# Row lists brought back in two parts by four transfers each, GpSimd's six positions nested, and the expert banks cleared ahead of the lists

## The reference, cut to what matters

```python
def moe_ffn(h, router_w, router_b, e_w_in, e_b_in, e_w_out, e_b_out):
    logits = xt @ router_w + router_b              # 32 experts
    top_v, top_i = lax.top_k(logits, 4)
    gates = jax.nn.softmax(top_v, axis=-1)
    # for every expert e, for the rows that chose it:
    #   hh = x @ e_w_in[e] + e_b_in[e];  gate, up = split(hh)
    #   act = min(gate, 7) * sigmoid(1.702 * min(gate, 7)) * (clip(up, -7, 7) + 1)
    #   y[row] += gate_of_row * (act @ e_w_out[e] + e_b_out[e])
x = layer_norm(alpha * x + mix);  x = layer_norm(alpha * x + moe_ffn(x))
```

## Time and profile before

| what | value |
|---|---|
| time, median of 3 runs | 1468.83 us (1467.07 to 1471.85) |
| time of the profiled execution | 1466.7 us |
| its span, first to last instruction | 1464.9 us |
| busy: PE / DVE / ACT / POOL | 1257.5 / 508.6 / 180.6 / 317.5 us |
| mean granted TensorE clock | 0.919 |
| DMA, mean over the span | 315 GB/s |

### The profile page before, as it was taken

The page is one execution under the profiler, slowest core; times in us unless marked ns, Lnnn a source line. Parts: engine busy times, 40 slices in busy tenths (PEclk is TensorE's granted clock), DMA queues, the critical chain, the costliest instruction groups (busy, mean ns, idle before and its releaser), DMA issues.

```text
span 1464.9 us, 32482 instructions
## 1 busy us (share of the span) xinstructions
PE 1257.5 (86%) x12135; PEld 558.0 (38%) x12136; DVE 508.6 (35%) x793; ACT 180.6 (12%) x358; POOL 317.5 (22%) x265
## 2 busy tenths in 40 slices
PE   6999978998378999999898989998999889997850
PEld 5876333555123333334223333344333323432220
DVE  2995431325632322222422222242222222423225
ACT  0003233012000100000110000011010000110012
POOL 7000132112321123112122222112113212120113
PEclk9999768887589999999999999999999999996985
DMA  9500441203489999999999999999999999999963
GB/s 344 164 3 22 166 118 64 94 30 130 196 330 414 418 410 401 405 416 408 409 414 416 406 411 402 409 388 401 418 415 398 409 414 408 379 402 418 407 220 117
DMA packets 86703, 461.27 MB, mean 315 GB/s; under 512 B 13360, under 2 KB 29325, under 8 KB 36753
## 3 DMA queue, kind: packets, MB, share of 16 engines
q1 hardware_dynamic: 67279, 433.61, 72.9%
q0 software_dynamic: 17136, 20.01, 6.0%
q10 hardware_dynamic: 2258, 7.26, 1.3%
HBM read 446.44 MB, written 19.47 MB: 318 GB/s over the span
## 4 chain that ended last, share of the span: by engine, by line
PE 64%; DMA 19%; DVE 8%; issue 6%; SPq 1%; ACT 1%; POOL 0%; POOLq 0%; DVEq 0%; ACTq 0%
PE pu L1599 30%; PE rest L1613 16%; DMA ring<-in_e_out 10%; DMA ring<-in_e_in 7%; DVE conv L1039 5%; PE pair L924 4%; PE pair L817 2%; PE pair L756 2%; PE pair L901 2%; PE pu L1593 1%; PE bS L882 1%; PE bS L871 1%; SPq L221 1%; DMA ring<-in_w_in 1%; PE bS L953 1%
## 5 line engine op out<-in xcount | busy, mean ns | idle before, releaser
L1599 PE MATMUL pu<-ring,xgT 128*32 128x512 f32 x5248 | 590.6, 603 | 39.5 <-DMA ring<-in_e_in 38.9
L1599 PEld LDWEIGHTS pu<-ring,xgT 128*32 128x32 f32 x5248 | 162.9, 111 | 449.5 <-issue 448.7
L1613 PE MATMUL rest<-ring,hid 128*32 128x256 f32 x5248 | 302.9, 387 | 24.1 <-DMA ring<-in_e_out 14.7
L1526 POOL DMA_INDIRECT acc_rows<-y,idx x82 | 129.6, 1581 | 764.8 <-ACT y L1660 732.8
L1739 DVE TENSOR_SCALAR gg<-pu 128x1280 f32<-128x1280 f32 x32 | 47.7, 1492 | 616.0 <-PE pu L1599 607.7
L1613 PEld LDWEIGHTS rest<-ring,hid 128*32 128x32 f32 x5248 | 172.9, 112 | 139.7 <-issue 42.1
L1652 ACT ACTIVATE ss<-gg 128x1280 f32<-128x1280 f32 x32 | 40.7, 1271 | 679.9 <-DVE gg L1739 679.9
L756 PE MATMUL pair<-xt,ring 128*128 128x260 f32 x448 | 100.6, 387 | 12.5 <-DMA ring<-in_w_in 12.5
L1517 POOL DMA_INDIRECT xq<-x_rows,idx x82 | 86.2, 1052 | 54.4 <-issue 42.8
L756 PEld LDWEIGHTS pair<-xt,ring 128*128 128x128 f32 x448 | 86.5, 193 | 25.7 <-DMA ring<-in_w_in 12.2
L1660 ACT ACTIVATE y<-rest,gate 128x256 f32 x160 | 61.8, 478 | 249.7 <-PE rest L1613 249.7
(11 more groups left out here) (256 smaller groups left out, 622.9 us busy)
## 6 DMA issues: line engine op xcount, KB each, us to landing
ring<-in_e_in SPq DMA_DIRECT2D x256, 1024.0 KB
ring<-in_e_out SPq DMA_DIRECT2D x128, 1024.0 KB
ring<-in_w_in SPq DMA_DIRECT2D x3, 1536.0 KB, 24.3
ring<-in_w_o SPq DMA_DIRECT2D x1, 4096.0 KB, 13.1
ring<-in_w_in SPq DMA_DIRECT2D x6, 512.0 KB, 12.4
xt<-in_xT SPq DMA_DIRECT2D x2, 1040.0 KB, 10.9
xtok<-in_x_prompt POOLq DMA_DIRECT2D x4, 512.0 KB, 3.8
x_rows<-conv ACTq DMA_DIRECT2D x4, 512.0 KB
```

The source lines that it names most:

```text
L1526: nc.gpsimd.indirect_dma_start(out=acc_quarters, out_offset=bass.IndirectOffsetOnAxis(ap=idx4[:, u % AHEAD, j:j + 1], axis=0), in_=y[:, u ...
L1599: mm = nc.tensor.matmul(pu[quarter(c), j], xgT[:, j, k], w[:, :, c * QC:(c + 1) * QC], start=False, stop=k == KT - 1, skip_group_check=True)
L1613: mm = nc.tensor.matmul(py[quarter(c), j], hid[:, j, 2 * q + f], w[:, f, c * QC:(c + 1) * QC], start=False, stop=q == FT // 2 - 1 and f == ...
```

## The change

It has four parts.

1. The lists come back by transfers of 32 partitions each. A first part (`0:NE * JG`, the first 160 pairs of each slot row) takes four transfers, two from SP and two from ACT; the rest takes four more from SP, with a semaphore of its own, `more_lists_in`. The list's order across is changed for that: all experts' first 5 groups stand first, then their second 5, and so on. VectorE's working out of the places (`stride`, `place_in_lists`) and of the block numbers (`job_rows`) follows.
2. `name_rows` for job 0 waits for the first part alone, and those for jobs 1 and 2 for the second as well.
3. `pu` and `py` are cleared before the wait for the lists, not after `name_rows`.
4. The six positions of a round of GpSimd's loop are nested: position i + 1 stands within the "is a job" of position i, and the gather's test within it too. The else branches go.

```diff
+    t = np.arange(1, MAXR)
+    put("stride", np.tile(1.0 - GS * NE * MAXQ + np.where(t % JG == 0, (NE - 1) * JG, 0), (P, 1)))
...
-            sp.dma_start(lists[:, :, :], lists_dram.unsqueeze(0).broadcast_to([NQ, GS, NE * MAXQ, 2])).then_inc(lists_in, 16)
+            for c in (0, 2):
+                sp.dma_start(lists[c * GS:(c + 1) * GS, 0:NE * JG], lists_dram[:, 0:NE * JG]).then_inc(lists_in, 16)
+            for c in range(NQ):
+                sp.dma_start(lists[c * GS:(c + 1) * GS, NE * JG:], lists_dram[:, NE * JG:]).then_inc(more_lists_in, 16)
...
             acc_store(NT)
+            a.wait_ge(listed, 16 * TOPK * (NT + 1))
+            for c in (1, 3):
+                a.dma_start(lists[c * GS:(c + 1) * GS, 0:NE * JG], lists_dram[:, 0:NE * JG]).then_inc(lists_in, 16)
...
-                ch.mark(V.scalar_tensor_tensor(flat4(spot[:, 0:n]), flat4(rank4[:, 0:n]), float(GS),
+                ch.mark(V.scalar_tensor_tensor(flat4(spot[:, 0:n]), flat4(rank4[:, 0:n]), float(NE * MAXN),
                                                flat4(chosen4[:, lo:hi]), ALU.mult, ALU.add))
+                ch.do(V.tensor_tensor(past[:, 0:n * TOPK], past[:, 0:n * TOPK],
+                                      C("stride").unsqueeze(1).broadcast_to([P, n * TOPK, MAXR - 1]), ALU.mult))
                 ch.do(V.tensor_reduce(flat4(wraps[:, 0:n]), past[:, 0:n * TOPK], AX.X, ALU.add))
-                ch.do(V.tensor_scalar(flat4(wraps[:, 0:n]), flat4(wraps[:, 0:n]), 1.0 - GS * NE * MAXQ, None, ALU.mult))
-                V.scalar_tensor_tensor(flat4(spots[:, lo:hi]), flat4(spot[:, 0:n]), float(MAXQ), flat4(wraps[:, 0:n]),
+                V.scalar_tensor_tensor(flat4(spots[:, lo:hi]), flat4(spot[:, 0:n]), float(JG), flat4(wraps[:, 0:n]),
                                        ALU.mult, ALU.add).then_inc(placed_in_lists, n)
...
-                ch.do(V.scalar_tensor_tensor(nth, exp, float(MAXN), nth, ALU.mult, ALU.add))
+                ch.do(V.scalar_tensor_tensor(nth, nth, float(NE), exp, ALU.mult, ALU.add))
...
-                for i in range(1, AHEAD + 1):
+                def place(i):
                     u = AHEAD * t + i
-                    with gp.If(u + 3 < last):
-                        ...
-                        gather(i + 3, size)
-                    with gp.Else():
-                        gp.nop()
                     with gp.If(u < last):
+                        with gp.If(u + 3 < last):
+                            ...
+                            gather(i + 3, size)
                         done, size = before(bass.ds(u, 1)), size_of(bass.ds(u, 1))
                         gp.wait_ge(scattered, 16 * done)
                         gp.sem_inc(y_free, 1)
                         gp.wait_ge(y_done, u + 3)
                         gp.sem_inc(gathers, 1)
                         scatter(i, size)
-                    with gp.Else():
-                        gp.nop()
+                        if i < AHEAD:
+                            place(i + 1)
+                place(1)
...
             choose(0)
-            d.wait_ge(lists_in, 16)
+            ch.mark(V.memset(pu[:, :, :, :], 0.0))
+            ch.mark(V.memset(py, 0.0))
+            d.wait_ge(lists_in, 16 * NQ)
             name_rows(ch, 0, 0)
+            d.wait_ge(more_lists_in, 16 * NQ)
             for u in (1, 2):
                 name_rows(ch, u, d.value_load(jobs[0:1, 2, u:u + 1], min_val=0, max_val=NE * MAXN - 1))
-            ch.mark(V.memset(pu[:, :, :, :], 0.0))
-            ch.mark(V.memset(py, 0.0))
             turn_rows(0, through(slice(1, 2)))
```

More of the change, by code:

```diff
@@ L83 @@
     ("diag", NH * NS), ("quarter", 1), ("part", NT + 1), ("tile0", NT + 1), ("exp", NE),
-    ("over", MAXN), ("job", 1), ("step", MAXR - 1), ("id32", GS), ("tie", NE), ("tie1", 1), ("place", NE)])
+    ("over", MAXN), ("job", 1), ("step", MAXR - 1), ("stride", MAXR - 1), ("id32", GS), ("tie", NE), ("tie1", 1), ("place", NE)])
 CHAN, NCHAN = _columns([("taps", 3 * TAPS), ("cb", 3), ("cg", 3), ("cbeta", 3), ("ps", 2)])
@@ L216, in layer @@
         lists_in = sem("lists_in")
+        more_lists_in = sem("more_lists_in")
         def load_unit(eng, e, j):
@@ L231, in first_block @@
         o[k] for k in "xT x_prompt x_sample w_in w_o cache_k cache_v state_pool state_conv".split())
-    ring, lists, lists_in, jobs, count, brow, C, load_unit = (
-        o[k] for k in "ring lists lists_in jobs count brow C load_unit".split())
+    ring, lists, lists_in, more_lists_in, jobs, count, brow, C, load_unit = (
+        o[k] for k in "ring lists lists_in more_lists_in jobs count brow C load_unit".split())
     x1_dram, acc_dram, lists_dram = o["x1_dram"], o["acc_dram"], o["lists_dram"]
@@ L1384, in moe_block @@
 def moe_block(nc, o):
-    ring, lists, lists_in, brow, jobs, count, C, sem, load_unit, unit_in = (
-        o[k] for k in "ring lists lists_in brow jobs count C sem load_unit unit_in".split())
+    ring, lists, lists_in, more_lists_in, brow, jobs, count, C, sem, load_unit, unit_in = (
+        o[k] for k in "ring lists lists_in more_lists_in brow jobs count C sem load_unit unit_in".split())
     x1_dram, acc_dram = o["x1_dram"], o["acc_dram"]
@@ L1547, in _ @@
             with gp.Fori(0, -(-MAXJ // AHEAD)) as t:
-                for i in range(1, AHEAD + 1):
+                def place(i):
                     u = AHEAD * t + i
-                    with gp.If(u + 3 < last):
[L1551 to L1555, removed]
-                        gather(i + 3, size)
-                    with gp.Else():
-                        gp.nop()
-                    with gp.If(u < last):
+                    with gp.If(u < last):
+                        with gp.If(u + 3 < last):
+                            done, size = before(bass.ds(u + 3, 1)), size_of(bass.ds(u + 3, 1))
+                            gp.wait_ge(named, u + 4)
+                            gp.wait_ge(gathered, 16 * done)
+                            gp.wait_ge(turned, u + 2)
+                            gp.sem_inc(gathers, 1)
+                            gather(i + 3, size)
                         done, size = before(bass.ds(u, 1)), size_of(bass.ds(u, 1))
```

## The result

The median is 1455.48 us (9 runs, 1450.97 to 1460.47) against 1467.07 us of the kernel before (9 runs on the same chip, 1463.83 to 1471.85): ratio 0.9916, 95% interval 0.9897 to 0.9934. The medians differ by 11.6 us; the ratios give 12.3 and 12.6 us (0.0084 and 0.0086 x 1467), so some 12.4. The forecast was 7.5 us and 1461.3 us, with a range from 1457.5: faster was right, the size was not. Of the 5.8 us between 1461.3 and 1455.48, 1.8 are the starting value (1468.83 in three runs, 1467.07 in nine); the other 4.1 are gain that the forecast did not have. Three slow executions (1743, 1898 and 6825 us, all in the set of e13 to e16) are left out of the ratios.

A forecast was written before the change was run, and what follows sets the result against it. The weight stream and its products were taken to hang on VectorE's first transposition. 1466.7 - 2.5 (head) - 5.0 (tail) = 1459.2 us, and 1461.3 as the runs' median, which is 2.1 higher; range 1457.5 to 1466.

The forecast's parts named there:

- What bounds the kernel: Whole kernel: weight loads and TensorE's products both hang on the end of VectorE's first transposition, at 404.48 us.
- theory D: Job stretch, written for the follow-up runs: the head's gain is eaten within the first jobs; e2 0 to 2 us faster.
- Issue and meeting, +0.2 us: Head: SP's six list issues take 2.5 us instead of 0.64, so the engines meet 0.2 us later.
- Landing: Head: first part of the lists there at 389 to 392 us, second at 391 to 395, before at 396.68.
- VectorE's naming: Head: job 0 is named once `pu` and `py` are cleared, at 395.3 us instead of 396.7, 1.4 us earlier.
- Gather and transposition: Head: job 0's rows land 4.8 us after naming; transposition starts at 400.4 us, not 403.0, 2.6 us earlier.
- Head, 2.5 us: Block change up to the first matmul: 2.6 us from the earlier transposition, less 0.1 for VectorE's added product.
- The clearing hides it: Head: lists there 3 to 6 us before naming; the clearing hides all but 1.4 of their some 7 us gain.
- The tail, 5.0 us: Last scatter to sums' load: nesting shortens GpSimd's 8.4 us walk to at most 2, so the scatter's landing ends it.
- Everything in the stream comes X earlier, since its rates and the ring are as before: Job stretch: a transposition X earlier moves the whole weight stream X earlier, with no gain or loss of its own.
- The sign of being wrong that I had named: Job stretch: forecast wrong if the stretch from first matmul to last scatter is not the same length as before.
- full gain of the lists: Head: naming follows the lists' landing at 390, head about 7 us, whole 12, 1456.5 us; chance 5 in 100.

The follow-up runs named there:

- e13: Kernel before with 16 unused columns ahead of `xgT`, behind `xq`, which stays in place: 1468.19 us, 1.0004 of the kernel before.
- e16: Same kernel as e8, measured again: 1451.82 us (6 runs), 0.9892 of the kernel before.
- e7: The change with `pu` and `py` cleared behind job 0's naming again, other parts kept: 1451.57 us, 0.9897 of the kernel before.
- e8: The change with `pu` cleared first, while the lists travel, and `py` behind job 0's naming: 1450.91 us, 0.9891 of the kernel before.
- e3: Kernel before with old lists, only `pu` and `py` cleared ahead of the wait for the lists: 1466.75 us, 1.0003.
- e1: Kernel before with only GpSimd's six loop positions nested: 1461.67 us, 0.9968.
- e9: The change, unaltered, measured a second time: 1454.92 us, 0.9914 of the kernel before.
- e4: Kernel before with the constants table 16 columns wider, which nothing reads: 1461.55 us, 0.9969.
- e5: Kernel before with an unused 16-column tensor behind the constants table, in SBUF alone: 1462.36 us, 0.9972.
- e12: Kernel before with 16 unused columns just ahead of `xq`, which then begins at byte 129,792: 1464.80 us, 0.9978.
- e17: Kernel before with 16 unused columns ahead of `xq` and 16 behind it, so `xq` alone is realigned: 1462.84 us, 0.9978.
- e10: The change with 16 more unused columns behind the constants table, putting `xq` at byte 129,856: 1458.30 us, 0.9938 of the kernel before.
- e2: Kernel before with only the new lists in two parts (and wider table), old loop, clearing behind the naming: 1457.54 us, 0.9938.

## Why the prediction was wrong, step by step

- **What bounds the kernel: right.** Loads and products hang on the first transposition. The ratios of e7, e8 and e16 against those of the change give the shorter head back at the end (theory D, that the gain is eaten on the way, falls).
- **Issue and meeting, +0.2 us: right, partly by luck.** VectorE's first operation is 3.63 us behind the lists' issue, against 3.41. SP's six issues took 2.9 us, where I had 2.5, but its drain took 0.13 us, where I had 0.46, and the two cancel. SP reached the meeting 0.1 us behind VectorE. In e8 an issue took longer and the meeting was 1.0 us late.
- **Landing: right, at the early end.** All lists were there 4.9 us behind their first issue; my 391 to 395 for the second part, counted from the issue at 386.26, are 4.7 to 8.7. The clearing hides it either way.
- **VectorE's naming: mis-sized by 0.5 us.** `pu` starts 0.53 us behind the cast, the same gap that the earlier trace rows shows ahead of `pu` and that I left out. Naming came 9.52 us behind the lists' issue, not 9.0.
- **Gather and transposition: right.** From naming to transposition 5.2 us, forecast 5.1.
- **Head, 2.5 us: right in sum, by two errors that cancel.** Against the one profile of the kernel before the head gained 2.06 us. But the old lists transfer took 10.42 us in that profile and 10.7 to 12.3 in the eleven other profiles of kernels that have it (mean of all twelve 11.3): I had the lowest of twelve, and that was luck. Against the mean head of those kernels with the old order, 20.0 us, the gain is 3.0 (mean of the change's three profiles 16.98).
- **"The clearing hides it": the mechanism right, a cost not seen.** I said that what is late next is the clearing. It is: undone (e7) the head is 3.2 us shorter. So the clearing ahead of the wait costs about 3 us beside the new lists, and nothing beside the old ones (e3).
- **The tail, 5.0 us: right.** 5.04, 5.08 (e1) and 5.15 us (e9), with the landing as the releaser. No branch waited for a fetch: the three tests (L1560) took 45 ns each and the walk was done 2.4 us behind the last scatter, within the landing's 3.7. (8.4 us over 17 positions are 0.49 us for each, not 0.45; it changes nothing here.)
- **"Everything in the stream comes X earlier, since its rates and the ring are as before": this is the step that failed.** The ring is; the rate is not. The sign of being wrong that I had named came true: from the first matmul to the last scatter it was 1015.3 us, not 1019.6. 16 columns in the constants table, which I priced nowhere, moved `xq` from 129,728 to 129,792, an odd multiple of 64 bytes to a multiple of 256, and the weights' packets went from 315.9 to 314.5 ns. Measured by itself, as medians apart: 5.2 (e4), 4.2 (e5), 2.6 (e12) and 3.8 us (e17), 4 us in the mean. (e4 and e5 move more tensors than e12 and e17 do; their packets are the same, and the difference in time is not clear of noise.) Taken out of the change, 3.4 us (e10 against e9). In my sum it stood at 0, and no bound of the range had a term for it.

The sum as it is now: 5.0 (tail) + 3.0 (head) + 4.0 (place of `xq`) = 12.0 us, against some 12.4 measured. The same terms, with the head of 13.80, give 15.2 us for e7, which measured 15.1 (0.0103 x 1467). Without the place, e10 has 9.1 us [7.2, 11.0], which holds both my 7.5 and the 8.0 of the mended two terms. The rival "full gain of the lists" (1456.5) was near in number and wrong in cause: naming did not follow the lists' landing. In e2 and e7 it does, nearly, and the head gains the 6.2 us that the clearing ahead otherwise takes half of.

What stays open: why a gather into the one place leaves the packets behind it short and into the other doesn't. The runs show that it is so for packets that go elsewhere, and for how long, but not in which part of the DMA path. Three places of `xq` were tried (129,728, 129,792 and 129,856), with one shape of gather: whether what counts is a multiple of 128, a multiple of 256 or something else of that one place isn't shown. An `xq` at 129,920 would tell the first two apart.

## What to carry to other kernels

In a kernel that a stream of DMA bounds, list what a change moves in SBUF, not only at its instructions: a table that grows shifts each tensor behind it, and a shift of 64 bytes was worth nearly as much here as the tail. Time an unused pad of the same size by itself before an edit's gain is put down to its idea. And when a wait is shortened, ask again whether what was put ahead to fill it still fits: the clearing that was free beside a transfer of 11 us cost 3 us beside one of 5.

## What the runs showed of the hardware that was not expected

- Weight packets of 8,192 bytes into tensors that don't move take 314.4 to 314.9 ns when the gathers' destination begins at byte 129,792 of a partition (ten kernels), and 315.7 to 316.4 ns when it begins 64 bytes below or above (nine kernels); nothing lies between.
- A transfer whose source is read four times over took 10.4 to 12.3 us for 640 KB in twelve executions; eight transfers with the same data were all there 4.9 us behind the first issue.
- A cast of 128 x 32 takes 1.91 us beside GpSimd's clearing of `xq` and 0.17 us behind it, while VectorE's clearing of `pu` takes 2.19 us with its first 1.3 us beside GpSimd's clearing (e8) and 2.19 us wholly behind it. So it matters what is put beside GpSimd's 2.23 us: the clearing of `pu` loses nothing there.
